# FFN 1's last projection as seven block products instead of eight

## The reference, cut to what matters

```
u = causal_dwconv(h @ w_up, dw_w)          # h 512 x 1024, w_up 1024 x 5632, 3 taps
a, v = split(u, 2)                         # 512 x 2816 each
y = (silu(a) * v) @ w_down                 # w_down 2816 x 1024
x = x + g_c * rms_norm(y, cm_post_g)
```

## Time and profile before

| what | us |
|---|---|
| median of 3 runs (lowest, highest) | 1629.88 (1629.34, 1637.10) |
| span of the profiled execution, first to last instruction | 1628.6 |
| TensorE busy | 1601.9 (98%) |
| VectorE, ScalarE, GpSimd busy | 931.5, 626.4, 188.0 |
| first matmul of FFN 1's down stage starts at | 776.97 |
| first matmul of block 2 starts at | 898.57 |

### The profile page before, as it was taken

The page is one execution under the profiler, slowest core; times in us unless marked ns, Lnnn a source line. Parts: engine busy times, 40 slices in busy tenths (PEclk is TensorE's granted clock), DMA queues, the critical chain, the costliest instruction groups (busy, mean ns, idle before and its releaser), DMA issues.

```text
span 1628.6 us, 20633 instructions
## 1 busy us (share of the span) xinstructions
PE 1601.9 (98%) x7892; PEld 1317.6 (81%) x7892; DVE 931.5 (57%) x1311; ACT 626.4 (38%) x826; POOL 188.0 (12%) x121
## 2 busy tenths in 40 slices
PE   6999999999999999999999999999999999999998
PEld 5888788788887888888888877778788888888887
...
GB/s 330 92 113 94 53 77 104 53 52 285 207 182 106 57 95 103 103 88 92 104 103 103 60 125 91 83 78 78 53 78 103 93 101 103 99 83 103 104 103 52
DMA packets 189159, 170.46 MB, mean 105 GB/s; under 512 B 9544, under 2 KB 176805, under 8 KB 189093
## 3 DMA queue, kind: packets, MB, share of 16 engines
...
HBM read 165.54 MB, written 2.10 MB: 103 GB/s over the span
## 4 chain that ended last, share of the span: by engine, by line
PE 92%; DVE 3%; ACT 2%; DMA 2%; issue 1%; SPq 0%; ACTq 0%; DVEq 0%
PE bank L1378 21%; PE bank L1380 20%; PE bank L1379 20%; PE bank L1393 7%; PE bank L1395 7%; PE bank L1394 7%; PE bank L1480 1%; PE bank L2011 1%; PE bank L1723 1%; PE bank L1386 1%; DMA w_raw<-in_w_in 1%; DVE w_lo L2068 1%; PE bank L1388 1%; PE bank L1387 1%; PE bank L1996 1%; DMA work<-in_ada_w 1%
## 5 line engine op out<-in xcount | busy, mean ns | idle before, releaser
L1378 PE MATMUL bank<-h_hi,w_hi 128*128 128x512 f32 (+1 forms) x1424 | 556.8, 391 | 2.8 <-DVE w_lo L2068 2.0
L1380 PE MATMUL bank<-h_hi,w_lo 128*128 128x512 f32 (+1 forms) x1424 | 548.7, 385 | 0.0
L1379 PE MATMUL bank<-h_lo,w_hi 128*128 128x512 f32 (+1 forms) x1424 | 548.0, 385 | 0.0
L2068 DVE TENSOR_TENSOR w_lo<-w_raw,w_hi 128x2048 fp32r<-128x2048 f32 x112 | 256.6, 2291 | 263.7 <-ACT w_hi L762 263.0
L762 ACT ACTIVATE w_hi<-w_raw 128x2048 fp32r<-128x2048 f32 x129 | 246.3, 1909 | 262.2 <-PE bank L1395 180.3
L1378 PEld LDWEIGHTS bank<-h_hi,w_hi 128*128 128x128 f32 x1424 | 267.6, 188 | 72.2 <-issue 16.1
L1380 PEld LDWEIGHTS bank<-h_hi,w_lo 128*128 128x128 f32 x1424 | 267.8, 188 | 54.2
L1379 PEld LDWEIGHTS bank<-h_lo,w_hi 128*128 128x128 f32 x1424 | 268.0, 188 | 52.1 <-issue 1.0
L1393 PE MATMUL bank<-w_hi,y_hi 128*128 128x512 f32 x352 | 137.8, 391 | 0.0
L1395 PE MATMUL bank<-w_lo,y_hi 128*128 128x512 f32 x352 | 137.0, 389 | 0.0
L1394 PE MATMUL bank<-w_hi,y_lo 128*128 128x512 f32 x352 | 137.0, 389 | 0.0
...
## 6 DMA issues: line engine op xcount, KB each, us to landing
w_raw<-in_w_in SPq DMA_DIRECT2D x94, 512.0 KB, 4.5
w_raw<-in_ffn_w_up SPq DMA_DIRECT2D x44, 512.0 KB, 5.0
w_raw<-in_w_up SPq DMA_DIRECT2D x44, 512.0 KB, 4.6
...
w_raw<-in_ffn_w_down SPq DMA_DIRECT2D x22, 512.0 KB, 4.0
w_raw<-in_w_down SPq DMA_DIRECT2D x22, 512.0 KB, 3.7
...
w_raw<-in_w_o SPq DMA_DIRECT2D x8, 512.0 KB, 4.4
```

Of the source, the lines that this page charges most:

```text
L1378: pe.matmul(dst, w_hi[s][:, at:at + n], hi, start=first, stop=False, skip_group_check=onto)
L1379: pe.matmul(dst, w_hi[s][:, at:at + n], lo, start=False, stop=False, skip_group_check=onto)
L1380: return pe.matmul(dst, w_lo[s][:, at:at + n], hi, start=False, stop=last, skip_group_check=onto)
L2068: dve.tensor_tensor(w_lo[u % 2][:, :], raw[u % 2][:, :], w_hi[u % 2][:, :].bitcast(FP32), ALU.subtract)\
```

## The change

With `A` the hidden activations and `B` the rows of `w_down`, hidden tiles 2j and 2j + 1, the two halves of the tokens and the two halves of the output columns make 2 x 2 blocks. The changed kernel computes the product by Winograd's form of Strassen's scheme, with seven block products instead of eight:

- Four products run in the first pass over 11 units (24 matmuls each), three in the second pass (18 each). Between the passes four PSUM banks are copied aside (`aside`) and combined (`between`), and the second pass goes on adding onto the results.
- The weight sums of the scheme are made by GpSimd within the up stage (`down_sums`, three additions for each of the 11 pairs), stored by SyncE in a DRAM tensor (`sums_store`), and loaded in the down stage (`down_rows`). `sums_load` brings the rows of `w_down` for them. Two slots in `work` hold them.
- The activation sums are made by VectorE (`hidden_sums`, `hidden_fourth`) and GpSimd (`inner_difference`).
- Four raw buffers instead of two serve the down stage's loads.
- The first transposes of rows (`rows_turned`) now stand behind all down matmuls.
- Semaphores are shared between FFN 1 and FFN 2 under new counts. FFN 2 computes what it did.

```diff
-                        ("wo", 4), ("up1", FT), ("down1", FT // 2),
+                        ("wo", 4), ("up1", FT), ("down1", FT),
...
+        raw_at = [raw[0], raw[1], area(FT * S + 4 * S, UNIT), area(FT * S, UNIT)]
+        def stage(j):
+            return area(FT * S + 10 * S + j % 2 * S, S)
+        def pair_of(j):
+            return area(j * 2 * S, 2 * S)
...
+        QUAD = S // 2
+        FIRST = ((0, 0, 0), (2, 1, 5), (1, 2, 1), (3, 3, 4))
+        kept = nc.dram_tensor("down_sums", (PAIR, P, 4 * S), FP32, kind="Internal").ap()
+        def sum_slot(p):
+            return area((18, 14)[p % 2] * S, 4 * S)
+        SECOND = ((1, 1, 0), (0, 2, 1), (2, 0, 4))
...
+                def sums_load(p):
+                    t, r = sum_slot(p), p * 2 * P
+                    if p >= 2:
+                        sp.wait_ge(sem(f"sums_kept{p % 2}"), 16 * (p // 2))
+                    else:
+                        sp.wait_ge(w_used, U["up1"] + 2)
+                    sp.dma_start(t[:, S:3 * S], w_down[r:r + P, :]).then_inc(sem(f"sums_in{p % 2}"), 16)
+                    sp.dma_start(t.rearrange("p (a n) -> p a n", a=4)[:, 0:4:3, :],
+                                 w_down[r + P:r + 2 * P, :].rearrange("p (a n) -> p a n", a=2)).then_inc(sem(f"sums_in{p % 2}"), 16)
+                def sums_store(p):
+                    sp.wait_ge(sem("sums_made"), 3 * p + 3)
+                    sp.dma_start(kept[p], sum_slot(p)).then_inc(sem(f"sums_kept{p % 2}"), 16)
+                if n == "1":
+                    for i in range(PAIR):
+                        for k in range(2):
+                            up_unit(i, k)
+                            p = 2 * i + k - 4
+                            if 1 <= p <= PAIR:
+                                sums_store(p - 1)
+                            if 0 <= p < PAIR:
+                                sums_load(p)
+                    return
...
+            def down_rows(w_down):
+                for g in range(FT):
+                    u, dst, r = DOWN + g, raw_at[g % 4], g % PAIR * 2 * P
+                    if g == 0:
+                        for k in range(2):
+                            sp.wait_ge(sem(f"sums_kept{k}"), 16 * ((PAIR + 1 - k) // 2))
+                    if g < 2:
+                        before(u)
+                    elif g == 3:
+                        sp.wait_ge(sem("hid"), FT + 1)
+                    elif g > 3:
+                        sp.wait_ge(parted[u % 2], u // 2 - 1)
+                    if g < PAIR:
+                        put(u, dst[:, 0:S], w_down[r:r + P, 0:S])
+                        put(u, dst[:, S:4 * S], kept[g][:, S:4 * S])
+                    else:
+                        put(u, dst[:, 0:S], kept[g - PAIR][:, 0:S])
+                        put(u, dst[:, S:3 * S], w_down[r + P:r + 2 * P, :])
+            down_rows(A["ffn_w_down"][0])
...
+                def tile(i, k):
+                    pool.wait_ge(sem("silu"), i * 2 + (BEFORE[n] * FT + k + 1))
+                    conv_done(k, 1, i)
+                    pool.tensor_tensor(work[:, bass.ds(i * (2 * S) + k * S, S)], cbuf[:, k, 0, :], cbuf[:, k, 1, :],
+                                       ALU.mult).then_inc(sem("hid"), 1)
+                pool.nop().then_inc(sem("hid"), 1)
+                if n == "2":
+                    with pool.Fori(0, PAIR) as i:
+                        for k in range(2):
+                            tile(i, k)
+                    return
+                def inner_difference(i):
+                    pool.wait_ge(sem("hid"), i * 2 + 3)
+                    b12, b22 = (work[:, bass.ds(i * (2 * S) + q * QUAD, QUAD)] for q in (1, 3))
+                    pool.tensor_tensor(b12, b12, b22, ALU.subtract).then_inc(sem("hid_e"), 1)
+                def down_sums(i, k):
+                    t, made = sum_slot(k), sem("sums_made")
+                    blocks = t.rearrange("p (a n) -> p a n", a=4)
+                    a11, x1 = (t[:, q * S:(q + 1) * S].unsqueeze(1).broadcast_to([P, 2, S]) for q in (1, 3))
+                    pool.wait_ge(sem(f"sums_in{k}"), i * 32)
+                    pool.tensor_tensor(t[:, 3 * S:4 * S], t[:, 2 * S:3 * S], t[:, 3 * S:4 * S], ALU.add).then_inc(made, 1)
+                    pool.wait_ge(made, i * 6 + (3 * k - 5))
+                    pool.tensor_tensor(blocks[:, 0:3:2, :], blocks[:, 0:3:2, :], a11, ALU.add).then_inc(made, 1)
+                    pool.wait_ge(made, i * 6 + (3 * k - 4))
+                    pool.tensor_tensor(blocks[:, 0:2, :], blocks[:, 0:2, :], x1, ALU.add).then_inc(made, 1)
+                def tiles_and_sums(i, sums):
                     for k in range(2):
-                        pool.wait_ge(sem("silu" + n), i * 2 + k + 1)
-                        conv_done(k, 1, i)
-                        pool.tensor_tensor(work[:, bass.ds(i * (2 * S) + k * S, S)], cbuf[:, k, 0, :], cbuf[:, k, 1, :],
-                                           ALU.mult).then_inc(sem("hid" + n), 1)
+                        tile(i, k)
+                        if k < sums:
+                            down_sums(i, k)
+                    inner_difference(i)
+                tiles_and_sums(0, 0)
+                with pool.Fori(1, 6) as i:
+                    tiles_and_sums(i, 2)
+                tiles_and_sums(6, 1)
+                for k in range(2):
+                    pool.wait_ge(sem(f"sums_kept{k}"), 16 * ((PAIR + 1 - k) // 2))
+                with pool.Fori(7, PAIR) as i:
+                    for k in range(2):
+                        tile(i, k)
+                    inner_difference(i)
...
+                def down_hi(g):
+                    act.wait_ge(loaded[g % 4], loaded_at(DOWN + g))
+                    act.wait_ge(w_used, DOWN + (g - 2 if g == FT - 2 else g - 1))
+                    dst, src = down_weights(w_hi, h_hi, g), raw_at[g % 4]
+                    if g < PAIR:
+                        ins = act.activation(dst[:, :], src[:, :], ACT.Copy)
+                    else:
+                        ins = act.activation(dst[:, 0:3 * S], src[:, 0:3 * S], ACT.Copy)
+                    ins.then_inc(hi_done, 1)
+                def hidden_hi(g):
+                    j = g % PAIR
+                    if g < PAIR:
+                        act.wait_ge(sem("hid_td"), 2 * j + 2)
+                    else:
+                        act.wait_ge(sem("down_lo1"), 2 * j + 2)
+                    if g >= 2:
+                        act.wait_ge(w_used, DOWN + (2 if g >= FT - 2 else max(g - 3, 0)))
+                    dst, pair = parts_at(y_hi, h_hi, g), pair_of(j)
+                    if g < PAIR:
+                        act.activation(dst[:, 0:S], pair[:, 0:S], ACT.Copy)
+                        ins = act.activation(dst[:, S:2 * S], stage(j), ACT.Copy)
+                    else:
+                        ins = act.activation(dst[:, 0:3 * QUAD], pair[:, QUAD:4 * QUAD], ACT.Copy)
+                    ins.then_inc(sem("down_hi1"), 1)
+                def aside(m):
+                    if m:
+                        act.wait_ge(w_used, DOWN + PAIR)
+                    else:
+                        act.wait_ge(sem("first_done"), 1)
+                    for c, dst in ((0, sq), (4, tbuf)):
+                        act.activation(dst[:, m, :], bank[T["down1"][c + 2 * m].bank][:, :], ACT.Copy).then_inc(sem("aside"), 1)
...
+                    down_hi(1)
+                    hidden_hi(2)
+                    hidden_hi(3)
+                    for g in range(1, FT - 1):
+                        if g == PAIR:
+                            aside(1)
+                        down_hi(g + 1)
+                        if g + 3 < FT:
+                            hidden_hi(g + 3)
+                        if g == PAIR - 1:
+                            aside(0)
+                    split(DOWN + FT)
...
+                def product(g, m, kinds):
+                    whole = g < PAIR
+                    w_h, w_l = down_weights(w_hi, h_hi, g), down_weights(w_lo, h_lo, g)
+                    p_h, p_l = parts_at(y_hi, h_hi, g), parts_at(y_lo, h_lo, g)
+                    for part, weight, c in kinds:
+                        t = T["down1"][c + 2 * m]
+                        if g == 0:
+                            wait_free(pe, t)
+                        if g == PAIR:
+                            pe.wait_ge(*{0: (sem("aside"), 2 * m + 1), 1: (sem("mid"), 4 * m + 3), 4: (sem("mid"), 4 * m + 4)}[c])
+                        a, b = part * QUAD + m * P, weight * S
+                        hi, lo = p_h[:, a:a + P], p_l[:, a:a + P]
+                        pe.matmul(bank[t.bank][:, :], hi, w_h[:, b:b + S], start=g == 0, stop=False, skip_group_check=True)
+                        pe.matmul(bank[t.bank][:, :], lo, w_h[:, b:b + S], start=False, stop=False, skip_group_check=True)
+                        mm = pe.matmul(bank[t.bank][:, :], hi, w_l[:, b:b + S], start=False, stop=not whole, skip_group_check=True)
+                        if g == FT - 1:
+                            done(mm, t)
```

(89 more changed lines are left out.)

103 lines of the change are left out of this document (68 added, 35 removed).

## The result

The changed kernel took **1654.24 us** (median of 4 runs, 1654.09 to 1655.66) against 1632.14 for the kernel before (4 runs, 1629.34 to 1637.1): ratio 1.0148, interval 1.0128 to 1.0168. The forecast was 1635.7, its range 1621 to 1649: the time lies above it. The profiled execution has a span of 1652.5 us (before 1628.6).

What follows compares the result with a forecast made beforehand. TensorE's matmul count and pace were taken to bound FFN 1. Terms -15.0 + 11.4 + 4.1 + 1.5 + 3.8 = +5.8 gave a span of 1634.4 and, with 1.3 for the median, 1635.7 us; range 1621 to 1649.

Steps and rivals of the forecast that it cites:

- the turnaround in the sums of the up stage: Up stage: SyncE's wake, issue, store and next load between two pairs' additions take 6.4 us, 6.0 to 7.0.
- 10 x loop - 115.6: Up stage: delay when store, load and additions loop slower than TensorE's 10.88 us; at 12.7 us a loop, +11.4 us.
- the loop is longer: Up stage rival: unhidden read opening and lo parts between additions, loop 13.35 to 14.5, total 1645 us; chance 0.22.
- The loop fits: Up stage rival: load overlaps store or GpSimd is quicker, loop under 11.6, up term 0, total 1624.3 us; chance 0.16.
- ScalarE's centre tap ... would cost if SyncE's list were mended: Up stage: its wait for a product behind additions is 5 us less late than the weights, so costs nothing beside them.
- VectorE against GpSimd: Up stage: lo parts and GpSimd's additions exclude each other at SBUF; without it the term would be about 3 us less.
- -14.96: Down stage: 66 of 528 matmuls removed at an unchanged pace of 0.2267 us, saving 14.96 us.
- Within the passes, 0: Down stage: VectorE and ScalarE prepare each unit within TensorE's time, by 0.5 us at least, so no cost.
- Start of the down stage, +4.1: Down stage's start: VectorE's lo parts make the second unit 3.1 us late and the third 1.0; ends 1.7 and 5.5.
- Between the passes, +1.5: Down stage's middle: bank combinations cost 0.5 us and the lo part behind them 1.0; ends 0.5 and 3.
- End, +3.8: Down stage's end: scaling, transposes and VectorE's row work delay block 2's first matmul by 3.8 us; ends 2.5 and 4.5.
- All is hidden but the end: Whole-kernel rival: the loop fits and the down stage's starts cost half, total about 1619.5 us; chance 0.09.

Runs made afterwards that it cites:

- e9_no_store: The changed kernel with sums made but not stored, SyncE still waiting for them before the next load, down stage reading w_down rows: 1626.74 us.
- e1_swap: The changed kernel with SyncE issuing each pair's load ahead of the store of the pair before: 1626.8 us, ratio 0.9983 to the kernel before.
- e11: e1_swap with hidden sums 2 and 3 and hidden lo part 3 moved, and the logarithm's table load ahead of the split: 1625.65 us, ratio 0.9980.

## Why the prediction was wrong

The mechanism was right, and one term of it was too small: **the turnaround in the sums of the up stage**, "I take 6.4", ends 6.0 and 7.0. It is 8.1. The text named the loop, its place in SyncE's list, the +11.4 by "10 x loop - 115.6" and what would show it. From 6.4 to 8.1 the loop goes from 12.7 to 14.35, and the same formula gives 27.9 for the unit that it speaks of, which started 28.1 late; the other 1.7 of the 29.9 are the low clock behind it. Point by point:

- *Turnaround.* The sum puts the store and the load one behind the other, each at its rate in mid-flow, and has no slow stretch beyond a possible opening of the load: the store 3.4 from issue to landing (0.7, 2.6, 0.1), the load 2.5 more. In the changed kernel a store lands 5.3 us after its issue, and the second load 2.8 after the store (631.4 against 628.6). So in that kernel the store's part is the one that was too small: the 2.6, scaled from the 1.35 of a 512 KB store, left out the slow tail. Taken alone the load's part was too small as well: 5.4 in e9_no_store against the sum's 3.8 (wake, issue, 2.5 of data, 0.1 to land, part of an opening). The guess that a store ahead hides the opening was right in kind, since the load behind the whole store opens fast; what it did not foresee is that the store then has a slow stretch of its own. A better reading was at hand: the very load of the earlier trace rows, 1 MB of w_down on an idle queue, was issued at 784.29 and landed at 789.15, 4.9 us later, where the parts of the sum give 3.3; and weights of 512 KB land 5.0 us after their issue.
- *GpSimd's additions*, 6.3 predicted, 6.26 measured. The guess that broadcast inputs cost nothing more holds (2.40 for 1024 elements, against 2.4 by the sum).
- *The rival "the loop is longer"* was closest: 13.35 to 14.5, 1642 to 1653 us. Its price was right, and its first cause in kind: a slow stretch that isn't hidden is paid in each turn, though behind the whole store it is the store's and not the read's opening. Its second, VectorE's lo part between the additions in many loops, was not: the second addition has a mean of 2.57 us over eleven pairs, and one of them took 4.33. I gave it 0.22 against 0.45. With ends at 6.0 and 7.0 for a queue state that no row showed, the term's own bounds were too tight; the formula multiplies their width by ten.
- *"The loop fits"* fell by the order of the list. That descriptors are taken in ring order, as the Trainium skill (DMA: Bandwidth & Descriptors, Queues, rings and completion order) says, agrees with the loads' landing: 7.2 us after issue behind the whole store, 5.9 behind half (median), 4.9 behind none; and with the packets above.
- *"ScalarE's centre tap ... would cost if SyncE's list were mended"*: it doesn't. In e1_swap the list is mended, and up is 217.73.
- *VectorE against GpSimd.* Right in kind: 4.33 for an addition of 2.4 where a lo part meets it, and in the changed kernel 3.02 in place of 2.29 for a lo part that waits for an addition (at 708.52). The Trainium skill's exclusive lock (SBUF — State Buffer, SBUF: two separate sides) agrees. On the path it is nothing once the list is in the right order.
- *Matmuls.* 66 fewer; -14.96 stands, as no unit of the down stage ran under its pace outside the seams. "Within the passes, 0" holds: between 825 and 870 us PE is busy without a gap at the clock 1.00.
- *Start of the down stage, +4.1.* A gap of 2.70 (predicted 3.1) and no second one, but the clock stood at 0.54 over 812.0 to 815.0 and at 0.94 over the next 5 us: 1.7 us lost. With 0.17 for the listing (next point) 4.6 together. In e1_swap the clock held and both gaps came (2.69, 0.79). The size was right, one half of the cause was not foreseen.
- *Between the passes, +1.5*: 0.24 and 0.60, and 0.17 more for each, since a gap is listed from a matmul's recorded end (0.39 us after its start, against a pace of 0.2267): 1.2, and 1.4 with the two matmuls behind the gaps, which take 0.1 longer. Right. Another 0.3 is lost at 909.7 to 910.1, which no term had.
- *End, +3.8*, ends 2.5 and 4.5: +5.1, outside its ends. (The text's own numbers, 5.9 against 2.0, give 3.9.) Two things were missed. ScalarE's split of the next weights waited 1.31 us for their load, and a table load of 1.28 us stood behind it, so block 0's squares began at 912.78; moving the table load gave back 0.5 (e11). And the transposes ran at a lower clock (0.76). With the -14.96 these terms make the stage's -3.5.
- *"All is hidden but the end", 1619.5.* The time doesn't follow from its words: -15.0, the end's 3.8 and half of 4.1 and 1.5 give 1621.5.
